# Two-block network on one core: order of ScalarE's work, a PSUM bank for one product, and the loads and first tokens of the start

## What is computed

```python
def first_block(...):                       # layers 0 and 1
    for i in range(2):
        m_lat = silu(c) @ w_mod[i] + b_mod[i]      # shift, scale, gate, twice
        m_ctx = silu(c_ctx) @ w_mod[i] + b_mod[i]
        u_lat = h_lat * (1 + scale) + shift        # u_ctx alike
        y = attention_mixer(u) if i == 0 else ssm_mixer(u)
        h_lat = layer_norm(ALPHA * h_lat + gate * y)
        f = square(relu(modulate(h_lat) @ w1)) @ w2
        h_lat = layer_norm(ALPHA * h_lat + gate2 * f)
def second_block(...):                      # layers 2 and 3
    # layer 2: Fourier and gated linear attention; layer 3: grouped attention
    a = rms_norm(h) * (1 + sc1) + sh1
    h = h + ga1 * mix(a)
    f = rms_norm(h) * (1 + sc2) + sh2
    h = h + ga2 * conv_ffn(f)     # (silu(g) * v) @ w_down, (g, v) = conv3(f @ w_up)
```

## Time and profile before

| | |
|---|---|
| median of 3 runs | 4260.65 us (4259.33 to 4261.77) |
| the profiled execution's own time | 4259.32 us |
| its span, first to last instruction | 4257.5 us |
| TensorE busy | 4039.0 us, 95% |
| VectorE busy | 1786.7 us, 42% |
| ScalarE busy | 815.5 us, 19% |
| mean granted TensorE clock | 0.98 |
| moved by DMA | 325.82 MB, mean 77 GB/s |

### The profile page before, as it was taken

How to read it: one execution, slowest core, us unless ns; L and a number is a source line. 1 busy time by engine, 2 the same in 40 slices (tenths; PEclk the granted TensorE clock), 3 DMA queues, 4 the chain that set the end, 5 groups by cost and what they waited for, 6 DMA issues and landing times.

```text
span 4257.5 us, 45853 instructions
## 1 busy us (share of the span) xinstructions
PE 4039.0 (95%) x18528; PEld 2498.0 (59%) x18528; DVE 1786.7 (42%) x3040; ACT 815.5 (19%) x1549; POOL 240.6 (6%) x228
## 2 busy tenths in 40 slices
PE   7999999999999999999999996799999999999999
PEld 5676588744455555558646545645555444758864
DVE  0254523100266655444102028736776015437841
ACT  1265111100112321111102022321100021531000
POOL 1000000000013441300000000000000000000000
PEclk9999999999999999999999997799999999999999
DMA  4255011211112211322223012301111112002222
GB/s 179 90 198 180 20 60 60 70 59 43 41 68 101 90 65 64 120 73 84 95 74 113 35 42 100 139 21 60 54 56 60 54 66 70 2 21 89 80 89 74
DMA packets 201230, 325.82 MB, mean 77 GB/s; under 512 B 4274, under 2 KB 90616, under 8 KB 200896
## 3 DMA queue, kind: packets, MB, share of 16 engines
q1 hardware_dynamic: 195136, 302.00, 20.6%
q0 software_dynamic: 5888, 20.91, 1.5%
HBM read 320.74 MB, written 2.16 MB: 76 GB/s over the span
## 4 chain that ended last, share of the span: by engine, by line
PE 88%; DVE 7%; ACT 3%; issue 1%; DMA 1%; POOL 0%; DVEq 0%; ACTq 0%; SPq 0%
PE PS L973 27%; PE PS L1013 22%; PE PS L948 3%; PE PS L1485 3%; PE PS L926 3%; PE PS L1064 3%; PE PS L1499 3%; PE PS L885 2%; PE PS L805 2%; PE PS L1486 1%; PE PS L1646 1%; PE PS L1178 1%; PE PS L1656 1%; PE PS L1337 1%; PE PS L1147 1%
## 5 line engine op out<-in xcount | busy, mean ns | idle before, releaser
L973 PE MATMUL PS<-RING,BIG 128*128 128x512 f32 x2352 | 1016.9, 593 | 3.7 <-DVEq L1713 1.6
L973 PEld LDWEIGHTS PS<-RING,BIG 128*128 128x128 f32 x2352 | 445.5, 190 | 557.1 <-issue 552.2
L1013 PE MATMUL PS<-UT,RING 128*128 128x256 f32 (+1 forms) x2432 | 648.2, 414 | 35.1 <-ACT BIG L2510 18.3
L1013 PEld LDWEIGHTS PS<-UT,RING 128*128 128x128 f32 x2432 | 461.3, 191 | 188.5 <-issue 25.3
L1013 PE MATMUL PS<-BIG,RING 128*128 128x256 f32 (+1 forms) x1824 | 487.6, 410 | 1.5 <-DVEq L1733 1.0
L1800 DVE TENSOR_TENSOR RES_TMP<-PS,GATE 128x512 f32<-128x512 f32 x80 | 55.3, 692 | 1030.2 <-PE PS L973 960.0
L1013 PEld LDWEIGHTS PS<-BIG,RING 128*128 128x128 f32 x1824 | 346.1, 190 | 107.1 <-DVEq L1733 3.1
L948 PE MATMUL PS<-RING,UT 128*128 128x512 f32 x320 | 141.1, 603 | 2.5 <-ACT BIG L2784 0.9
L973 PE MATMUL PS<-RING,UT 128*128 128x512 f32 x320 | 139.2, 593 | 2.0 <-issue 1.2
L1485 PE MATMUL PS<-UT,RING 128*128 128x512 f32 x256 | 132.4, 599 | 3.8 <-issue 3.1
L2493 ACT ACTIVATE UT<-PS,COL 128x128 f32<-128x128 f32 x328 | 119.1, 468 | 75.6 <-PE PS L863 73.3
(11 more groups left out here) (403 smaller groups left out, 4686.3 us busy)
## 6 DMA issues: line engine op xcount, KB each, us to landing
RING<-w_mod_dram SPq DMA_DIRECT2D x48, 2048.0 KB, 8.0
RING<-w_ffn_up_dram SPq DMA_DIRECT2D x44, 1024.0 KB, 5.0
RING<-ff_w_dram SPq DMA_DIRECT2D x32, 1024.0 KB, 5.4
RING<-ff_w_dram SPq DMA_DIRECT2D x16, 2048.0 KB, 7.8
RING<-ssm_w_in_dram SPq DMA_DIRECT2D x8, 2048.0 KB, 7.8
RING<-w_ffn_down_dram SPq DMA_DIRECT2D x8, 1536.0 KB, 6.6
RING<-w_ffn_down_dram SPq DMA_DIRECT2D x8, 1280.0 KB, 5.7
RING<-ssm_w_out_dram SPq DMA_DIRECT2D x4, 2048.0 KB, 7.8
```

What stands on the lines that cost most here:

```text
L973: m = mm(bank(t), inp[:, kk, t * 128:(t + 1) * 128], w[:, k, :], start=kk == 0, stop=kk == kn - 1)
L1013: m = mm(bank(bank_, n), a[:, k, :], b[:, k, :], start=k == 0, stop=k == 3)
```

## The change

It has four parts.

1. `boundary`: in layers 0 and 1 ScalarE takes the turned tile t-1 before the root of tile t, and not after it. Layers 2 and 3 had that order.
2. `product_banks` gives a fourth bank, `bd`: 6 for even pairs and 7 for odd ones in layers 1 to 3, and the old bank in layer 0. The sixth product goes there, without waiting for `quarters_taken` + 3; in the first two pairs it waits until the last turned tile was taken. Product 1 of a pair waits for quarter 3 of the pair two before, and not 5. VectorE takes the sixth product from `bd`.
3. POOL waits for `x` before it issues the bias and the context, and until three weight tiles were used before it issues the attention constants.
4. Tokens 0 and 1 are turned within the modulation, behind the third weight tile, in banks 0 to 3. Tokens 2 and 3 follow in banks 4 to 7 after the bias columns, and the first attention products start with 256 columns, then 128 and 128, with the context's turning after the third piece.

```diff
 def product_banks(L, p):
-    return ((0, 2, 3), (1, 4, 5))[p % 2] if tiles_of(L)[0] == NT else ((4, 0, 1), (5, 2, 3))[p % 2]
+    if L == 0:
+        return ((0, 2, 3, 0), (1, 4, 5, 1))[p % 2]
+    return ((0, 2, 3, 6), (1, 4, 5, 7))[p % 2] if L == 2 else ((4, 0, 1, 6), (5, 2, 3, 7))[p % 2]
...
 def modulation_start(L):   # TensorE
                     if m:
                         mod_columns(L, m - 1, 7, MOD_ROWS_START[:, (m - 1) % 2, :])
+                    if L == 0 and m == 2:
+                        turn_tokens(0, "m", 0, "tokens_turned", 0)
+                        turn_tokens(0, "m", 1, "tokens_turned_too", 2)
...
 def one(p):
-                        pe.wait_ge(S("quarters_taken"), 7 * (n0 + p - 2) + 5)
+                        pe.wait_ge(S("quarters_taken"), 7 * (n0 + p - 2) + (3 if L else 5))
...
 def seven_three_four(p):
                     done(product(bb, s3, t3))
-                    pe.wait_ge(S("quarters_taken"), 7 * (n0 + p) + 3)
-                    done(product(ba, s4, b22))
+                    if L == 0:
+                        pe.wait_ge(S("quarters_taken"), 7 * (n0 + p) + 3)
+                    elif p < 2:
+                        seen(L, "f", ntok - 1)
+                    done(product(bd, s4, b22))
...
 def mixer0():   # TensorE
-                for t in range(TL):
-                    turn_tokens(0, "m", t, *(("tokens_turned", 6), ("tokens_turned_too", 4))[t % 2])
+                turn_tokens(0, "m", 2, "tokens_turned", 4)
+                turn_tokens(0, "m", 3, "tokens_turned_too", 6)
...
-                early_tile(0, "m", t0, f, None, 2, [(0, 256, 2), (256, 256, 3)], [(LAT, 128, 4), (LAT + 128, 128, 5)], {(0, 1): context})
+                seen(0, "m", 0)
+                early_tile(0, "m", t0, f, None, 2, [(0, 256, 1), (256, 128, 2), (384, 128, 3)], [(LAT, 128, 4), (LAT + 128, 128, 5)], {(0, 2): context})
...
 # VectorE, a pair, and the start of layer 0
-                    take(V.tensor_tensor(q12, q22, bank(ba, n), ALU.add))
+                    take(V.tensor_tensor(q12, q22, bank(bd, n), ALU.add))
...
+                    offer(flow(0, "tokens_turned_too", 1))
+                    dve.wait_ge(S("tokens_in"), 16)
+                    post("m_tokens_ready", TL)
+                    modulation(L)
+                    turned_tokens((1,))
                     dve.wait_ge(S("tokens_in"), 32)
-                    post("m_tokens_ready", NT)
-                    modulation(L)
-                    turned_tokens((1, 3, 5))
+                    post("m_tokens_ready", TC)
+                    turned_tokens((3, 5))
...
 def boundary(L, which):   # ScalarE
                     for t in range(ntok):
-                        if L >= 2:
-                            if t:
-                                turned_(t - 1)
-                            rms(L, "f", t, "m_residual_ready", tiles_before(L, "f"))
-                            continue
-                        root(L, which, t)
                         if t:
                             turned_(t - 1)
+                        if L < 2:
+                            root(L, which, t)
+                        else:
+                            rms(L, "f", t, "m_residual_ready", tiles_before(L, "f"))
...
 # POOL
-            bring("tokens_in", H[:, TL:NT, :], d["ctx"][0].rearrange("(t p) n -> p t n", p=128))
+            pool.wait_ge(S("tokens_in"), 16)
...
             bring_bias(layers[0])
+            bring("tokens_in", H[:, TL:NT, :], d["ctx"][0].rearrange("(t p) n -> p t n", p=128))
...
                 if L == 0:
+                    pool.wait_ge(wused, 3)
                     bring("attention_constants_in", A_CONST, d["c_att"])
```

More of the change, by code:

```diff
@@ L1019, in one @@
                 def one(p):
-                    ba, _, _ = product_banks(L, p)
+                    ba, _, _, _ = product_banks(L, p)
                     a11, _, _, _ = weight_blocks(weights(t0 + p))
                     if p >= 2:
-                        pe.wait_ge(S("quarters_taken"), 7 * (n0 + p - 2) + 5)
+                        pe.wait_ge(S("quarters_taken"), 7 * (n0 + p - 2) + (3 if L else 5))
                     else:
@@ L1035, in six_and_five @@
                 def six_and_five(p):
-                    _, bb, bc = product_banks(L, p)
+                    _, bb, bc, _ = product_banks(L, p)
                     s1, s2, _, _ = weight_sums((t0 + p) % 2)
@@ L1047, in seven_three_four @@
                 def seven_three_four(p):
-                    ba, bb, _ = product_banks(L, p)
+                    _, bb, _, bd = product_banks(L, p)
                     _, _, _, a22 = weight_blocks((t0 + p) % 2)
@@ L1772, in turned_tokens @@
                 f = flow(0, "tokens_turned_too", 1)
-                offer(f)
                 for t in tiles:
@@ L1777, in turned_tokens @@
                     for k in range(KD):
-                        step.go(V.tensor_scalar(UT[:, k, t * 128:(t + 1) * 128], bank(4, 128, k * 128), COL[:, 1, k, p:p + 1], COL[:, 0, k, p:p + 1], ALU.mult, ALU.add))
+                        step.go(V.tensor_scalar(UT[:, k, t * 128:(t + 1) * 128], bank(2 if t == 1 else 6, 128, k * 128), COL[:, 1, k, p:p + 1], COL[:, 0, k, p:p + 1], ALU.mult, ALU.add))
                     step.settle()
@@ L2369, in paired_up @@
                 for p in range(PAIRS[L]):
-                    ba, bb, bc = product_banks(L, p)
+                    ba, bb, bc, bd = product_banks(L, p)
                     q11, q12, q21, q22 = quarters(L, p)
@@ L2484, in gate_rows, with turned_tokens @@
                 post("gate_rows_ready")
-            def turned_tokens(L, which, t):
+            def turned_tokens(L, which, t, b=6):
                 f = flow(L, "tokens_turned", 1)
@@ L2492, in turned_tokens @@
                 for k in range(KD):
-                    step.go(A(UT[:, k, t * 128:(t + 1) * 128], bank(6, 128, k * 128), ACT.Identity, scale=COL[:, w + 1, k, p:p + 1], bias=COL[:, w, k, p:p + 1]))
+                    step.go(A(UT[:, k, t * 128:(t + 1) * 128], bank(b, 128, k * 128), ACT.Identity, scale=COL[:, w + 1, k, p:p + 1], bias=COL[:, w, k, p:p + 1]))
                 step.settle()
@@ L2503, in first_product @@
             def first_product(L, p):
-                n, (ba, _, _) = 128 * half_tiles(L), product_banks(L, p)
+                n, (ba, _, _, _) = 128 * half_tiles(L), product_banks(L, p)
                 _, q12, _, _ = quarters(L, p)
@@ L2948, in _ @@
             act.wait_ge(S("eps_ready"), 1)
+            offer(flow(layers[0], "tokens_turned", 1))
             modulation_start(layers[0])
@@ L2951, in _ @@
                 if L == layers[0]:
-                    offer(flow(L, "tokens_turned", 1))
                     offer(flow(0, "q", 4))
@@ L2955, in _ @@
                     for t in (0, 2, 4):
-                        turned_tokens(L, "m", t)
+                        turned_tokens(L, "m", t, 4 if t else 0)
                 (mixer0, mixer1, mixer2, mixer3)[L]()
```

4 lines of the change are left out of this document (2 added, 2 removed).

## The result

The changed kernel took 4229.04 us (median of four runs, 4225.04 to 4231.82) against 4259.99 for the kernel before in the same session (four runs, 4255.01 to 4261.77): a ratio of 0.9929 with a 95% interval of 0.9911 to 0.9946, or 31 us less. The prediction was 4222.5 us with a range of 4214 to 4236. The profiled execution took 4230.08 us with a span of 4228.3, 29.2 us shorter than the span before (4257.5).

The account below looks back on a forecast made before the run. TensorE, busy for 95% of the span, was taken as the bound, so time could come only from its idle and slow stretches. Start 5.0, order 9.0, its price -0.5 and bank 24.5 sum to 38.0 us: 4222.5 us, range 4214 to 4236.

Parts of the forecast that it names:

- the rival of the clock: Boundaries and start: shorter waits near 2.2 us still halve TensorE's clock, taking back 4.5 + 1.5 us, about 4228.5; chance 0.14.
- Own bank: Fourier and last layers' pairs: the sixth product no longer waits for VectorE to free its bank; 24.5 us, bounds 16 to 26.
- The rival in which the wait moves on: Convolving layers: VectorE is the bound and the seventh product's quarter is late; some 5 of 24.5 us stay, 4242; chance 0.08.
- ScalarE ahead of the root: Last tile, attention and state-space layers: taking before the root brings the sixth product 4.7 and 4.3 us earlier; together 9.0.
- the root is at 501.1 (0.3 late): Attention layer's last tile: after taking tile 4 until 501.0, ScalarE does tile 5's root at 501.1, against 500.80 before.
- The price of the order: 12 earlier tiles: the root waits for a taking, norms end 1.2 us later, just in time; cost 0.5 us, bounds 0 and 4.
- The rival of a root too late: The norm misses the transposes at all 12 tiles: 4234, or 4300 if the clock halves behind each wait; chance 0.03.
- Start: Kernel start up to the attention products: earlier weight loads 4.0 us and token order net 0.9; 5 us, of 2.5 to 8.
- The loads' term: Start: keeping context and attention constants off the lines brings the modulation weights earlier; 4.0 us, of 2 to 6.
- the fourth tile lands near 32.8: Start: the fourth modulation weight tile lands near 32.8 us, not 37.1; bounds 31.8 and 35.
- The tokens' steps: Start: the first 256 columns need only tokens 0 and 1, so the second taking's wait of 1.8 us goes; net 0.9.
- The narrow pieces: First attention products: cutting 256 columns into two of 128 makes 128 records of 64; cost 0.9 us.

Follow-up runs that it names:

- the split of the sums: Changed kernel with VectorE's four sums of weights split, two behind the norm of the tile before, two behind the last norm: 4222.95 us, ratio 0.9914; second run 4223.15, 0.9917.
- context later: Changed kernel with the context asked for when the third modulation tile is used, ahead of the attention constants, not behind the bias: 4229.17 us, ratio 0.9927.
- turned early: Changed kernel with tokens 0 and 1 turned behind the second modulation tile, not the third: 4227.79 us, ratio 0.9918.
- all three edits: Changed kernel with the sums of weights split, tokens 0 and 1 turned one tile earlier and the context asked for later: 4223.08 us, ratio 0.9911.
- old loads: Changed kernel with x, context and attention constants asked for together at the start, without GpSimd waits between them, as in the kernel before: 4228.93 us, ratio 0.9923.

## Why the prediction was right, and where it was not

The forecast (faster, 38.0 us) was right in sign and range, and 7 us too good. Its mechanisms held; two of its terms were too large, and the range had room for that because the rival of the clock was put inside it. That rival's time, 4228.5 us, is nearer to the 4229.04 measured than the forecast's 4222.5, and that is luck in part: the clock was half of what the boundaries lacked, and VectorE's queue, which no rival named, the other half.

**Own bank, 24.5 us: right.** 12.1 forecast and 12.1 measured in the Fourier layer (8.4 and 3.7), 12.2 forecast and 12.6 measured in the last (8.2, 2.0 and 2.0). The pitch of 12.1 us and VectorE's 0.2 us of slack are what the trace after shows. The rival in which the wait moves on is out.

**ScalarE ahead of the root, 9.0 us: the mechanism right, the size 5.3.** The step that failed is "the root is at 501.1 (0.3 late)". The new order does move each norm 1.2 us later, and I counted that for the norm and its transposes at the tiles before, where it costs nothing, as forecast. But behind the norm of the last tile but one, on VectorE, stand four sums of weights and then the gate and the variance of the last tile. They move by the same 1.2 us, and the root waits for the variance. I followed the moved norm to TensorE and not down its own engine's queue. That is 0.9 us at each boundary; the split of the sums gave 0.95 of each wait back. The other 0.9 at each is the clock: in the kernel with the context later, the second product behind the same 3.10 us ran at full speed, and the attention layer's stretch took 13.8 us in place of 14.8. The rival "the clock takes part back" had the chance of 0.14, on one row each way (2.26 us did, 2.02 did not), and its bound of 4.5 us for the two boundaries is nearer to what came than the 9.0 I took. A term of 4.7 us that hangs on the clock behind a wait of about 2 us should have been put in the middle.

**The price of the order, 0.5: 0.4 at most.** Just in time meant in time: TensorE's first weights of the transposes stand idle for 0.24 us ahead of them, as the weights of the products beside them do, and the pitch does not change. The rival of a root too late is out.

**Start, 5.0 us: 4.2, and differently made.** The loads' term was 4.0 us, but its own steps gave less: rows of the fourth tile that begin near 34.7 and take 2.0 to 3.3 us end at 36.7 to 38.0, and against the 40.4 of the profile before that is 2.4 to 3.7 us. In the six profiles with the start's change and no more they begin at 35.0 to 36.7 and end at 37.0 to 38.7, 37.5 of mean, against 40.4, 40.7 and 39.3 in the three without it: 2.6 us. The step that failed is "the fourth tile lands near 32.8". The bytes did end there (the lines fall quiet at 33.0), but the tile counts as landed, and TensorE can use it, only at 34.8 to 35.1; it landed at 36.9 to 37.2 in the three profiles without the change, so it came 2.1 us earlier and not 4.3. In the changed kernel's first profile the third tile adds to that: its rows, at the lower clock level, last until 33.6, and the transposes behind them until 36.7.

The tokens' steps held: from the last step of the columns (line 849) to the first product it takes 7.6 us and not 9.5 (forecast 1.8 less, measured 1.9). The narrow pieces cost less than the 0.9 forecast. From the first product to the 512-column ones it takes 44.6 us of mean and not 44.2; where the first records run at the full level in both, it is 44.15 (turned early, all three edits) against 43.74 (before, order alone): 0.4 us. The kernel with the old loads says how far the tokens alone go. Its line 849 is at 40.3, against 41.4 of mean in the three without the change: 1.2 us that I had not seen, since its rows behind the transposes run at the full level (1.96 us), where two of those three took 3.23 and 3.64 behind a wait. So the tokens are worth some 2.3, and the loads some 1.9 of the 4.0, just under the lower bound of 2.

The Trainium skill (TensorE: Matmul & The Clock Gate, Part 4: PE-mode transpose) says that transposes do not count as busy for the clock, and by that the fourth tile's rows behind them would have stayed slow. In the eight profiles in which they stand directly behind the transposes of tokens 0 and 1 (changed kernel three times, start alone, sums split twice, context later, old loads), they took 1.95 to 1.96 us, the full level, each time; the rise came ahead of the transposes or within them (16 of them in 2.93 us, 1.91 where the clock was up throughout). That does not show that transposes count: 2.7 to 3.6 us of matrix products stand right ahead of them in each. It shows that the consequence I drew, rows at the lower level and 1.3 us less, does not follow.

**The clock at the last layer** was no term of the sum at all, and took 1.7 us in the profile after: its second product behind 2.02 us of idle is at the lower level in twelve of fourteen profiles, and the kernel before, whose one profile I read, was one of the two where it is not. The kernel with the bank alone shows it too, as does the one with the start alone, so no single part brings it; whether the kernel has to do with it at all is not shown.

The sum by stretches: 24.7 for the bank, 5.3 for the order, 4.2 for the start, less 1.7 for the last layer's first pair and 1.5 in all other stretches, 31.0 us, against the 31 of the medians. The start is a mean over profiles in it and the rest comes from one profile each way, where the start is 2.5 and the sum the 29.2 of the spans; so the close fit is in part luck. The 1.5 in the other stretches has no cause shown, and single profiles of one kernel differ by as much there.

## What to carry to other kernels

When an instruction moves, follow its delay down the queue of its own engine until something waits for what stands behind it, and not only along the data it produces: here 1.2 us of a norm became 0.9 us of TensorE through four additions that had nothing to do with it. A wait for a buffer that recurs in every pair is worth a bank of its own where the engine that frees it still has idle time in the loop: here VectorE's 1.02 us of idle in 12.93 said that its own work would fit the shorter pitch, and the 24.5 us forecast came as 24.7. When a queue of loads is reordered, the gain is set by the last load on the path and by what is asked for next; asking for the context later moved the third tile by 3 us and the 512-column products by nothing.

## What the runs showed of the hardware

The same idle time of TensorE, 3.1 us at the same two places in seven profiles, was followed once by the full clock throughout and thirteen times by slower products; 2.02 us by the full clock in two profiles of fourteen. Waits of 1.86 us never lost it, in 40 places. A forecast from one profile's clock behind a wait between 2 and 3 us can fall either way, and so can a comparison of two single profiles: the start of one and the same kernel came out at 92.7, 90.0 and 90.6 us, mostly by where the clock was up: in the third tile's rows (3.64, 3.22 and 3.64 us; 1.96 at the full level), the 16 transposes behind them (2.93, 1.91 and 1.91) and the first 48 attention records (8.18, 7.32 and 7.60). A 2 MB tile of weights counted as landed 1.8 to 2.1 us after the lines had fallen quiet (33.0, and 34.8 with the tokens turned early, 35.1 in the changed kernel).
